# Four edits to a two-block kernel: a filter weight laid over 128 partitions, a first product taken term by term, a weight split moved amid the convolutions, four square sums on VectorE

## What is computed

```python
# first block
h = rms_norm(x);  z, xbc, dt, q, k, v, g_ssd, g_att = split(h @ w_in)        # 1024 x 7440
xbc = silu(causal_dwconv(xbc, conv_w, conv_b))                                # 4 taps
y = ssd(xbc, dt) ; yg = (y * silu(z)) in 2 groups of 512
y_ssd = rms_norm(yg, per group) @ w_ssd_out                                   # sums of squares by row and group
y_att = attention(rope(q), rope(k), v) @ w_attn_out
x = x + (sigmoid(g_ssd) * y_ssd + sigmoid(g_att) * y_att) @ w_out
x = x + mixture_of_experts(rms_norm(x))       # 32 experts, each 3 weights of 1 MB, 2 chosen for a row
x = x + sigmoid(rms_norm(x) @ w_ple_gate) * (p @ w_ple) ; x = rms_norm(x) * final_norm_w
# second block
h = rms_norm(x);  proj = h @ w_in_2
filters = sin(freq_2*(sin(freq_1*(z @ w_f1 + b_f1)) @ w_f2 + b_f2)) @ w_f3    # 256 x 33 -> 64 -> 64 -> 2048
u_hy = two gated long convolutions of three short-convolved parts, by the filters' spectra
u_attn = latent attention with 8 heads
x = x + (gate_hy * (u_hy @ w_hy_out) + gate_attn * (u_attn @ w_attn_out)) @ w_out_2
```

## Time and profile before

| | us |
|---|---|
| median of 3 runs | 804.8 (803.48 to 805.18) |
| profiled execution, its time | 803.98 |
| profiled execution, its span from first to last instruction | 802.2 |
| PE busy in it | 738.8 (92%) |
| DVE busy | 465.1 (58%) |
| ACT busy | 321.8 (40%) |

### The profile page before, as it was taken

The page is one execution under the profiler, slowest core; times in us unless marked ns, Lnnn a source line. Parts: engine busy times, 40 slices in busy tenths (PEclk is TensorE's granted clock), DMA queues, the critical chain, the costliest instruction groups (busy, mean ns, idle before and its releaser), DMA issues.

```text
span 802.2 us, 11034 instructions
## 1 busy us (share of the span) xinstructions
PE 738.8 (92%) x4636; PEld 560.0 (70%) x4636; DVE 465.1 (58%) x825; ACT 321.8 (40%) x479; POOL 17.9 (2%) x15
## 2 busy tenths in 40 slices
PE   7999999989999999996799797689999999799998
PEld 7978876878877885553245353348999966578886
DVE  6878965545766756432242131048588799845673
ACT  6464437436437325210110010047755623255631
POOL 0000000000000000000000000001100003000000
PEclk9999999999999999998889899999999999999999
DMA  9755542233439759899999999995563643523211
GB/s 319 245 203 171 177 158 93 94 106 107 152 115 405 271 223 421 321 370 421 421 421 421 420 421 420 418 395 174 183 221 131 215 157 106 157 105 105 105 52 53
DMA packets 63153, 189.97 MB, mean 237 GB/s; under 512 B 7481, under 2 KB 11835, under 8 KB 51132
## 3 DMA queue, kind: packets, MB, share of 16 engines
q1 hardware_dynamic: 61326, 184.44, 61.1%
q10 hardware_dynamic: 1774, 4.79, 1.9%
HBM read 188.16 MB, written 1.05 MB: 236 GB/s over the span
## 4 chain that ended last, share of the span: by engine, by line
PE 57%; DVE 17%; DMA 16%; ACT 7%; issue 2%; POOL 0%; SPq 0%; ACTq 0%; DVEq 0%
PE pb L519 53%; DMA WHo<-in_w_exp_up 7%; DMA raw<-in_w_exp_up 6%; DVE rawo L1785 5%; PE pb L528 4%; ACT WH L1282 3%; DMA WHo<-in_w_exp_down 2%; DVE cv_ L1892 1%; ACT arena L1441 1%; DMA raw<-in_w_in 1%; DVE arena L2051 1%; DVE arena L1838 1%; ACT arena L1310 1%; DVE HTl L1819 1%; POOL small L2684 0%
## 5 line engine op out<-in xcount | busy, mean ns | idle before, releaser
L1785 DVE TENSOR_TENSOR rawo<-raw,WH 128x2048 fp32r<-128x2048 f32 (+5 forms) x80 | 172.7, 2175 | 71.1 <-ACT WH L1282 71.1
L519 PE MATMUL pb<-WH,HTh 128*128 128x512 f32 (+2 forms) x384 | 155.8, 406 | 5.9 <-ACT arena L1310 3.2
L1282 ACT ACTIVATE WH<-raw 128x2048 fp32r<-128x2048 f32 (+5 forms) x80 | 144.1, 1823 | 20.9 <-PE pb L519 15.1
L519 PE MATMUL pb<-rawo,HTh 128*128 128x512 f32 (+2 forms) x384 | 148.3, 386 | 0.0
L519 PE MATMUL pb<-WH,HTl 128*128 128x512 f32 (+2 forms) x384 | 148.2, 386 | 0.0
L519 PEld LDWEIGHTS pb<-WH,HTh 128*128 128x128 f32 x384 | 72.8, 190 | 24.7 <-issue 5.1
L519 PEld LDWEIGHTS pb<-rawo,HTh 128*128 128x128 f32 x384 | 72.6, 189 | 14.4
L519 PEld LDWEIGHTS pb<-WH,HTl 128*128 128x128 f32 x384 | 72.9, 190 | 13.2 <-issue 1.0
L519 PE MATMUL pb<-raw,arena 128*32 128x256 f32 (+1 forms) x256 | 49.8, 484 | 13.4 <-DMA raw<-in_w_exp_up 8.1
L519 PE MATMUL pb<-WH,arenao 128*128 128x512 f32 x192 | 59.6, 391 | 1.2 <-DVE arenao L1819 1.2
L519 PE MATMUL pb<-arena 128*32 128x256 f32 (+6 forms) x252 | 58.7, 432 | 1.6 <-ACT arena L1698 0.7
(11 more groups left out here) (363 smaller groups left out, 1260.6 us busy)
## 6 DMA issues: line engine op xcount, KB each, us to landing
raw<-in_w_in SPq DMA_DIRECT2D x46, 1024.0 KB, 4.9
raw<-in_w_exp_up SPq DMA_DIRECT2D x18, 1024.0 KB, 21.5
arena<-in_w_exp_gate SPq DMA_DIRECT2D x13, 1024.0 KB, 23.3
arena<-in_w_exp_down SPq DMA_DIRECT2D x12, 1024.0 KB, 17.5
WHo<-in_w_exp_down SPq DMA_DIRECT2D x9, 1024.0 KB, 23.0
raw<-in_w_out SPq DMA_DIRECT2D x8, 1024.0 KB, 5.3
raw<-in_w_exp_gate SPq DMA_DIRECT2D x8, 1024.0 KB, 15.9
WHo<-in_w_exp_up SPq DMA_DIRECT2D x8, 1024.0 KB, 20.9
```

The lines of the kernel that those rows point to most:

```text
L519: return e.matmul(o, l, r, start=start, stop=stop, skip_group_check=True)
L1282: e.activation(h_, r_, ACT.Copy).then_inc(hi.sem, hi.mark(k))
L1785: e.tensor_tensor(l_, r_, h_.bitcast(F32), ALU.subtract).then_inc(lo.sem, lo.mark(k))
```

## The change

- `FW`, the last filter weight (64 x 2048, 512 KB), is laid over 128 partitions of 1024 columns: partitions 0 to 63 take the left half of the columns, 64 to 127 the right half. So that the hidden rows stand in both halves, `f1` and `f2` are loaded twice side by side, the filter's hidden tile `FH` has 128 partitions, and the biases in `rows2` are loaded twice (four more small transfers on SP's queue). `kernel_rows` takes its operands from the partitions of its half.
- The product of the left half of w_ple_gate (`gemm_by_part` for `gemm`) takes its first tile term by term: high x high for four chunks, then low x high, then high x low; it waits for each part only ahead of its term. The second tile is taken as before.
- ACT splits tile 7 (the second tile of q) after the second tap of the second group of convolutions, ahead of the first silu of that group, instead of after the group.
- All four sums of squares ahead of the transposes of y are on DVE; ACT has none.

```diff
--- before.py
+++ after.py
@@ -223,7 +223,7 @@
 
         anw, mnw, snw, gw, sums = (sm(8) for _ in range(5))
         rows = arena[:, 16896:17024]
-        rows2 = sb("rows2", [4, 64])
+        rows2 = sb("rows2", [4, 128])
         rows3 = sb("rows3", [18, 128])
         posi = sm(2, dt=I32)
         dtb, alog, dsk = sm(16), sm(16), sm(16)
@@ -231,7 +231,7 @@
         gcq, gckv = sm(3), sm(2)
         gqr, gkr = sm(32), sm(32)
         colp = sm(114)
-        col2 = sm(4, parts=64)
+        col2 = sm(4)
         col3, pair = sm(18), sm(1, parts=96)
         st = [sm(8) for _ in range(2)]
         norm_of = {n: st[(i + 1) % 2] for i, n in enumerate(("n1", "ssd", "nm", "np", "nf", "ng", "cq", "ck"))}
@@ -307,12 +307,12 @@
         KR = arena[:, 4096:6144].rearrange("p (f d) -> p f d", f=2)
         KI = arena[:, 8704:10752].rearrange("p (f d) -> p f d", f=2)
         PX = [[arena[:, o:o + 512] for o in (14656, 17216)], [rt_[:, o:o + 512] for o in (1024, 1536)]]
-        FW = arena[0:64, 15168:17216]
+        FW = arena[:, 15168:16192]
         PN = arena[:, 17216:17728].rearrange("p (t d) -> p t d", t=2)
         fw = arena[:, 17728:18752]
-        f1 = arena[0:33, 18752:18816]
-        f2 = arena[0:64, 18816:18880]
-        FH = arena[0:64, 14656:15168].rearrange("p (a l) -> p a l", a=2)
+        f1 = arena[0:33, 16192:16320]
+        f2 = arena[0:64, 16320:16448]
+        FH = arena[:, 14656:15168].rearrange("p (a l) -> p a l", a=2)
         PT_ = arena[:, 8192:8704].rearrange("p (c l) -> p c l", c=2)
         SG = sg_[:, :].rearrange("p (a l) -> p a l", a=2)
         T0, T1 = SG[:, 0, :], SG[:, 1, :]
@@ -544,6 +544,24 @@
                 for c in range(len(chunk_at[key])):
                     gemm_chunk(name, key, c, o, lhs, ready)
 
+            def gemm_by_part(name, key, lhs, ready, drainers):
+                o = [ring.take((name, t), drainers[t]) for t in range(2)]
+                k = chunk_at[key][0][0]
+                w = tile_parts(k)
+                for l, r in ((0, 0), (1, 0), (0, 1)):
+                    (hi, lo)[r].wait_ge(e, k)
+                    for c in range(4):
+                        if l:
+                            ve.wait_ge(e, (ready, c))
+                        else:
+                            ac.wait_ge(e, (ready, "hi", c // 2 * 2))
+                        for t in range(2):
+                            ins = mul(o[t][:, :], lhs[l][:, c, t * 128:t * 128 + 128], w[r][:, c, :],
+                                      c == 0 and l == r == 0, False)
+                ins.then_inc(mm.sem, mm.mark(("tile", k)))
+                for c in range(4, 8):
+                    gemm_chunk(name, key, c, o, lhs, ready)
+
             open_fill, fill_at = {}, deque([6])
 
             def fill(n):
@@ -939,13 +957,14 @@
 
             def filter_layer(n, wgt, src):
                 o = ring.take(("fh", n), ve)
-                mul(o[0:64, 0:256], wgt, src).then_inc(mm.sem, mm.mark(("fh", n)))
+                mul(o[:, 0:256], wgt, src).then_inc(mm.sem, mm.mark(("fh", n)))
 
             def kernel_rows(n):
                 o = ring.take(("kf", n), ve)
                 ac.wait_ge(e, ("fh", 1))
-                mul(o[:, :], FH[:, 1, (n // 4) * 128:(n // 4) * 128 + 128],
-                    FW[:, (n % 4) * 512:(n % 4) * 512 + 512]).then_inc(mm.sem, mm.mark(("kf", n)))
+                rows_, col = slice(64 * (n % 4 // 2), 64 * (n % 4 // 2) + 64), 512 * (n % 2)
+                mul(o[:, :], FH[rows_, 1, (n // 4) * 128:(n // 4) * 128 + 128],
+                    FW[rows_, col:col + 512]).then_inc(mm.sem, mm.mark(("kf", n)))
 
             def spectrum(s):
                 m0, m1_, o_, i = SPECTRA[s]
@@ -1038,7 +1057,7 @@
                 if q == 1:
                     d_late.wait_ge(e, "in")
                     o = ring.take("col2", ve)
-                    turn(o[0:64, 0:4], rows2[:, :])
+                    turn(o[:, 0:4], rows2[:, :])
                     turn(o[:, 4:22], rows3[:, :]).then_inc(mm.sem, mm.mark("col2"))
                 if q == 3:
                     for n in range(4):
@@ -1053,7 +1072,7 @@
                 down(q)
                 if q == 2:
                     ac.wait_ge(e, ("fh", 0))
-                    filter_layer(1, f2[:, :], FH[:, 1, :])
+                    filter_layer(1, f2[:, :], FH[0:64, 1, :])
                 if q == 3:
                     for n in range(4, 8):
                         kernel_rows(n)
@@ -1069,7 +1088,7 @@
                 ve.wait_ge(e, ("x moe", 1, j // 4))
 
             transposed("np", lambda t: X[:, t, :], 8, rows="(c p)", ready=moe_half)
-            gemm(("wpg", 0), ("wpg", 0), NT, "np", (ac, ac))
+            gemm_by_part(("wpg", 0), ("wpg", 0), NT, "np", (ac, ac))
             right = [ring.take((("wpg", 1), t), ac) for t in range(2)]
 
             def gate_rows(t, chunks):
@@ -1383,6 +1402,8 @@
                     e.activation(dtT, pb("dtT")[0:16, 0:256], ACT.Copy).then_inc(ac.sem, ac.mark("dtT"))
                 for n, g in enumerate(gs):
                     tap(g)
+                    if i == 1 and n == 1:
+                        weights(chunk_at[("cx", 2)][0][0] + 1)
                     if n:
                         convolved(gs[n - 1])
                 convolved(gs[-1])
@@ -1476,12 +1497,6 @@
                 e.activation(gv, gv, ACT.Sigmoid).then_inc(ac.sem, ac.mark(("gate 1", i)))
 
 
-            ss = norm_of["ssd"]
-            for i in (0, 2):
-                ve.wait_ge(e, ("yz", i // 2, i % 2))
-                mm.wait_ge(e, ("y", 1, 1))
-                e.activation(yjunk[i], yparts[i], ACT.Square, accum_out=ss[:, i:i + 1]).then_inc(
-                    ac.sem, ac.mark(("sq", i)))
             weights(used(("wao", 0)))
             ve.wait_ge(e, "yn")
             d_late.wait_ge(e, "in")
@@ -1583,7 +1598,9 @@
                     cst2, flat = A["cst2"], lambda n: A[n].rearrange("a k n -> (a k) n")
                     for cut in (slice(0, 1024), slice(1600, cst2.shape[1])):
                         e.dma_start(c2[:, cut], cst2[:, cut]).then_inc(d_c2.sem, d_c2.mark("in", by=16))
-                    for dst, src in ((FW, flat("w_f3_2")), (f1, flat("w_f1_2")), (f2, flat("w_f2_2")),
+                    for dst, src in ((FW, A["w_f3_2"].rearrange("a k (h n) -> (a h) k n", h=2)),
+                                     (f1[:, 0:64], flat("w_f1_2")), (f1[:, 64:128], flat("w_f1_2")),
+                                     (f2[:, 0:64], flat("w_f2_2")), (f2[:, 64:128], flat("w_f2_2")),
                                      (PN, A["p"].rearrange("a b (t p) d -> p (a b t) d", p=128))):
                         e.dma_start(dst, src).then_inc(d_filt.sem, d_filt.mark("in", by=16))
                     e.dma_start(hyb, A["hy_bias_2"].rearrange("a o n -> a (o n)")).then_inc(
@@ -2103,10 +2120,10 @@
 
             ss = norm_of["ssd"]
             ve.wait_ge(e, ("yz", 1, 1))
-            for i in (1, 3):
+            mm.wait_ge(e, ("y", 1, 1))
+            for i in range(4):
                 e.tensor_tensor_reduce(yjunk[i], yparts[i], yparts[i], 1.0, 0.0, ALU.mult, ALU.add,
                                        ss[:, i:i + 1]).then_inc(ve.sem, ve.mark(("sq", "ssd")))
-            ac.wait_ge(e, ("sq", 0), ("sq", 2))
             ve.wait_ge(e, ("sq", "ssd"))
             scale_of("ssd", ss[:, 0:4], 512)
             po.wait_ge(e, ("rs", "ssd"))
@@ -2322,7 +2339,7 @@
             def filter_phase(n):
                 mm.wait_ge(e, ("fh", n))
                 ve.wait_ge(e, "col2")
-                e.tensor_scalar(FH[:, 0, :], pb(("fh", n))[0:64, 0:256], col2[:, 2 * n:2 * n + 1],
+                e.tensor_scalar(FH[:, 0, :], pb(("fh", n))[:, 0:256], col2[:, 2 * n:2 * n + 1],
                                 col2[:, 2 * n + 1:2 * n + 2], ALU.add, ALU.mult).then_inc(
                     ve.sem, ve.mark(("fha", n)))
                 ve.wait_ge(e, ("fha", n))
@@ -2355,7 +2372,7 @@
                     ranks(q // 2 + 2)
                 if q == 1:
                     mm.wait_ge(e, "col2")
-                    e.tensor_copy(col2, pb("col2")[0:64, 0:4])
+                    e.tensor_copy(col2, pb("col2")[:, 0:4])
                     e.memset(pair, 1.0)
                     e.tensor_copy(col3, pb("col2")[:, 4:22]).then_inc(ve.sem, own("col2"))
                     ve.wait_ge(e, "col2")
@@ -2774,8 +2791,8 @@
                              (rows3[8:16, :], A["final_norm_w"].rearrange("(j p) -> j p", p=128)),
                              (rows3[16:17, 0:96], A["g_qn_2"]), (rows3[17:18, 0:96], A["g_kn_2"]),
                              (rows3[16:17, 96:128], A["g_qn_2"][:, 0:32]), (rows3[17:18, 96:128], A["g_kn_2"][:, 0:32]),
-                             (rows2[0:1, :], A["b_f1_2"]), (rows2[1:2, :], A["freq_1_2"]),
-                             (rows2[2:3, :], A["b_f2_2"]), (rows2[3:4, :], A["freq_2_2"])):
+                             *((rows2[i:i + 1, o_:o_ + 64], A[n]) for o_ in (0, 64)
```

(1 more changed line is left out.)

## The result

The changed kernel takes 809.2 us (median of 20 runs, 807.05 to 810.67), the kernel before 805.5 (20 runs on the same chip, 803.48 to 808.57). The ratio is 1.0043, with a 95% interval of 1.0033 to 1.0053: 3.5 us slower, 2.7 to 4.3. The forecast was 813, 8.2 us above the median of before that it started from, or 8.9 us on the profiled execution. The profiled execution took 808.03, its span is 806.2, and its mean granted clock is 0.966 of full speed (0.974 before).

The account below looks back on a forecast made before the run. Limits differ by stage: DMA saturated at 421 GB/s from about 330 to 530 us, PE nearly continuous before and after. Terms -1.8 - 1.6 + 0 + 12.3 = +8.9 us gave 812.9, stated as 813; range 799 to 818.5.

Parts of the forecast that it names:

- rival (1): Expert stage: the filter transfer runs on two engines, which hold back later tiles; 807.4 to 817.3 us, chance 0.72.
- the price of the filter transfer: Expert stage: two engines' lag of 15.5 us less 3.2 us paid before, net +12.3 us.
- lower bound: Filter transfer's net price of +6.8: two engines at 26.3 GB/s each, 10.0 us against 3.2 before.
- half rate: Filter transfer: two engines' writes meet others' at the same partitions and run at half rate, 19.9 us.
- The alternation of FW's rows with tile rows: Expert stage: on two engines FW's 64 rows alternate with tile rows, taking 30 to 40 us from about 350.
- The split amid the convolutions: Near 49 us: ACT's half of tile 7 fills an idle hole, PE's wait goes; gain 1.8 us, bounds 0 and 1.9.
- The four squares: Near 240 to 248 us: all four on DVE let PE's transposes start sooner; gain 1.6 us, bounds 1.2 and 1.7.
- The product by term: First w_ple_gate product, near 540 us: starts 1.2 us sooner off the chain; 0, bounds -0.6 and +0.3.
- Extra small transfers, doubled weights, 128 columns: SP's and ACT's queues and the filter's products: all costed at 0; bounds -0.3 and +0.3 for weights and columns.
- Filter inputs late for PE: Before the filter's first product: inputs land near 390 to 400, PE's extra stall is a few us beside tile waits.
- The half rate of 64 partitions: Filter transfer: 64 partitions take bytes at half the rate of 128, losing 2.0 us that full-rate 128 would regain.

Follow-up runs that it names:

- e2: The kernel before with the filter edit alone (FW over 128 partitions, on two engines): 812.3 us, ratio 1.0093 to the kernel before.
- e1: The changed kernel with the filter edit taken back (FW on 64 partitions), the other three edits kept: 800.8 us, ratio 0.9947 to the kernel before.
- e3: The changed kernel with FW loaded by two transfers of 64 rows, shared by 16 engines: 800.9 us, ratio 0.9952 to the kernel before.
- e6: The changed kernel with FW, still on two engines, issued last of the filter's transfers and waited for a quarter later: 810.6 us, ratio 1.0069 to before.
- e5: The changed kernel with half of FW's bytes on two engines, the other half in two transfers of 64 rows: 806.6 us, ratio 1.0019 to before.
- e9: The changed kernel with half of FW's bytes on two engines, all of FW issued last and waited for a quarter later: 805.5 us, ratio 1.0005.
- e8: The kernel before with only the first product of w_ple_gate taken term by term: 806.0 us, ratio 1.0013 to the kernel before.
- e12: e3 with the first product of w_ple_gate as it was before, not term by term: 801.3 us, ratio 0.9946 to the kernel before.
- e10: The changed kernel with FW on two engines issued last, hyb ahead of the other filter inputs, PE waiting at its first filter layer: 810.8 us, ratio 1.0064.
- e4: The kernel before with only the split of tile 7 moved amid the convolutions: 804.2 us, ratio 0.9988 to the kernel before.

## Why the prediction was wrong

**Direction and mechanism were right, one size was not.** The forecast's rival (1), two engines, is what happened; the step that failed is the price of the filter transfer, "I take a value nearer the upper end, 15.5 us". Net of 3.2 it made +12.3; the stage grew by 7.25 (after), 7.16 (e2), and the medians give 7.7 (after's ratio less e1's, 0.96%) and 7.5 (e2). That is close to the lower bound, +6.8, which held the two engines at their full rate of 26.3 GB/s and no meeting at the partitions. That the measured time lies inside rival (1)'s own range, 807.4 to 818, is owed to this lower bound, not to the value chosen. With 7.25 in place of 12.3 the sum is 803.98 - 3.4 + 7.25 = 807.8; the profiled execution took 808.03.

**No half rate.** The packet records of the traces show it directly (the last column is the time of all of FW's packets, divided by the number of engines):

| | FW's packets | time of one, median | sum by engine |
|---|---|---|---|
| before | 64 of 8 KB, 16 engines | 0.50 us | 2.0 us |
| e3 | 128 of 4 KB, 16 engines | 0.22 us | 1.8 us |
| after | 128 of 4 KB, two engines | 0.168 us | 11.0 us |
| e6 | 128 of 4 KB, two engines | 0.180 us | 11.7 us |

For comparison: in after 128 packets of 4 KB of the constants, on ACT's queue just ahead of FW, took 0.162 us each, and the tile packets of 8 KB 0.31 at 400 to 420 us. So FW's packets on two engines ran at 96% of that rate in after and 90% in e6. Their neighbours, the tile packets, took 0.33 us in the median while FW passed in after, and 0.51 in before. The half rate is what all 16 engines on 64 partitions show, and I had carried it over to the neighbours of two.

With the measured packets the price comes out: 11.0 - 3.2 = 7.8 us for 7.1 measured (after), 11.7 - 3.2 = 8.5 for 8.9 (e6). Packets of half the bytes are dearer for their size: the 2 KB packets of e5 and e9 took 0.10 us each, 64 of them 6.4 to 6.5 us on each of the two engines. With 1.6 for the other half of FW (half of 3.2) that is 6.5 + 1.6 - 3.2 = 4.9, for 5.2 and 5.4. These are estimates from packets and rows; they hit all four within 0.7 us. (With 1.25 us deducted, the bytes alone, after would come to 9.8.) The alternation of FW's rows with tile rows was forecast at 30 to 40 us, and took 30.6.

**The split amid the convolutions**: forecast -1.8; PE gained 2.0 on arrival at 162 us, the split alone measured -1.0 (0 to -1.9). In after 1.3 us of it went back to the lower clock in the next product, as in part or whole in eight of the ten profiled executions with the split. That wait and its clock weren't in the sum.

**The four squares**: forecast -1.6, measured -1.4 (-2.2 to -0.6), and the place looks as told. Both together: forecast -3.4, e1 -4.3 (-5.6 to -2.9). The sum of the two comes close in e1, though the parts alone gave only -2.4, so some of this agreement may be luck.

**The product by term**: forecast 0 with a longer wait ahead of 556; 0 in its own place, in after and in e8. Whether e8's +1.0 in whole time is real, e12 against e3 is too coarse to say.

**Extra small transfers, doubled weights, 128 columns**: forecast 0; e3 has them all and is level with e1 within the intervals.

**Filter inputs late for PE**: forecast "near 390 to 400", they landed by 390.0, and the wait cost nothing, as e10 against e6 shows. Not forecast at all was ACT stuck in its issues for 24 us and PE idle for 17 behind it. It cost no net time: in e6 the stall is gone and the time isn't better, and in e9 the stage isn't shorter than in e5. That the two engines were behind all the same is the likely reason. Whether it would have cost something alone at this length was not tried.

**The half rate of 64 partitions**, 2.0 us to be regained: not seen, since e3 still writes 64 at a time.

**Open**: FW issued first is 1.8 us cheaper in the stage than issued last (after and e2 against e6 and e10; 0.21 to 0.26% by the medians). The two engines' own packets took 0.7 us less in after than in e6 (11.0 for 11.7); the other 1.1 us no run separates. For half the bytes the order makes no difference.

## What to carry to other kernels

Look at the outermost dimension of both sides of a transfer, not only at its bytes: a view that reads well in the code (two halves of 64 rows) can put 0.5 MB on two engines, and in a saturated stream every later tile waits for them. If the shape can't be changed, cut the transfer (two calls of 64 rows, e3, gave back 7 us). Price such a lag at the engines' own full rate less what the transfer cost before, and look at the time of single packets before adding contention for which there is no row.

## What was not expected of the hardware

- An engine that issues transfers can itself be held by a transfer with few engines: with FW first, ACT's issues took up to 10.5 us each, 24 us in all. They took 4.5 us with FW on 16 engines (e3) and 3.9 with FW last (e6).
- Two engines that wrote to 128 partitions beside 14 busy ones kept nearly their full rate (0.168 us for a packet of 4 KB in after, where the constants' took 0.162), where 16 writing to 64 partitions took 0.50 us for 8 KB in place of 0.31, and fell to 256 GB/s.
- After the same wait of 2.0 us, the same six matmuls took 0.39 or 0.63 us each, that is the one or the other clock level, in executions of kernels that arrive there within 0.1 us of each other (e4 at 162.71, after at 162.76): 1.3 us, as much as one of the edits is worth.
- The stream's buffers hid a PE stall of 12.6 us, all but 0.6 to 1.0 us of the stage, which is near the spread of the stage's length (0.85 us over seven kernels).
